# RWKV-7 chunk step of a hybrid decoder: chunk matrices as 64-wide blocks on 64x64 array tiles, and the rotation behind the state update

## The reference

```python
p = p + (shifted - p) * mu                  # shifted: the token before, or the stored state
r, k, v, wl, al, gl = jnp.split(p, B_SPLITS, axis=-1)
w = -jax.nn.softplus(-(w0 + jnp.tanh(wl) @ w2)) - 0.5
decay = jnp.exp(-jnp.exp(w))
a = jax.nn.sigmoid(a0 + al @ a2)
g = jax.nn.sigmoid(gl) @ g2
kk = heads(k * k_k); kk = kk / norm(kk)
k = k * (1.0 + (a - 1.0) * k_a)
b_h = kk * a_h

def step(S, inp):
    r_t, d_t, k_t, v_t, kk_t, b_t = inp
    sa = jnp.einsum('bhij,bhj->bhi', S, -kk_t)
    S = S * d_t[:, :, None, :] + sa[..., None] * b_t[:, :, None, :] + v_t[..., None] * k_t[:, :, None, :]
    return S, jnp.einsum('bhij,bhj->bhi', S, r_t)
```

## Time and profile before

| | |
|---|---|
| median of 3 runs | 3579.61 us |
| the profiled execution's own time | 3578.4 us |
| its span | 3576.6 us |
| granted TensorE clock over the span | 0.969 of full |
| PE busy / DVE / ACT / POOL | 94% / 50% / 33% / 5% |
| HBM traffic | 137 GB/s over the span |

### The profile page before, as it was taken

One profiled execution on the slowest core, in us unless ns is written; L12 is line 12 of the kernel. 1 busy time (PEld: TensorE's weight loads), 2 busy tenths in 40 slices (PEclk: granted clock), 3 DMA queues, 4 the chain that ended last, 5 costly groups with the idle time before them and its releaser, 6 DMA issues.

```text
span 3576.6 us, 57327 instructions
## 1 busy us (share of the span) xinstructions
PE 3367.3 (94%) x23190; PEld 3156.5 (88%) x23190; DVE 1802.5 (50%) x2295; ACT 1192.8 (33%) x1553; POOL 162.1 (5%) x253
## 2 busy tenths in 40 slices
PE   8997888889999999999999978788999999999998
PEld 7996865579999999999999967555999999999998
DVE  5337665145545454454543476742555554545444
ACT  3223117533332232232432231364333233223224
POOL 1002011000000000000000020210000000000000
PEclk9998979999999999999999988799999999999999
DMA  6660005676555555554565500167655555555554
GB/s 190 161 149 5 1 2 197 256 173 146 152 153 143 151 153 139 157 152 137 147 174 151 113 1 1 40 224 263 141 152 152 149 139 159 146 139 161 145 144 128
DMA packets 846373, 490.57 MB, mean 137 GB/s; under 512 B 96352, under 2 KB 822896, under 8 KB 845808
## 3 DMA queue, kind: packets, MB, share of 16 engines
q1 hardware_dynamic: 845804, 488.85, 49.0%
q10 hardware_dynamic: 452, 0.11, 0.0%
HBM read 480.79 MB, written 8.12 MB: 137 GB/s over the span
## 4 chain that ended last, share of the span: by engine, by line
PE 86%; DVE 7%; ACT 3%; issue 1%; DMA 1%; SPq 0%; ACTq 0%; DVEq 0%
PE PS L1317 83%; PE PS L1318 3%; ACT ktr L823 1%; DMA cV<-in_cache_a_v 1%; DVE xm L1022 0%; ACT psm L794 0%; DVE psm L1192 0%; DVE WT L1084 0%; DVE hl L1257 0%; DVE WT L1085 0%; ACT ppt L805 0%; DVE S0T L1171 0%; DVE S0P L1145 0%; DVE nm L1194 0%; DVE xm L1027 0%
## 5 line engine op out<-in xcount | busy, mean ns | idle before, releaser
L625 ACT ACTIVATE wh<-raw 128x2048 fp32r<-128x2048 f32 (+1 forms) x408 | 711.7, 1744 | 1286.0 <-PE PS L1317 1249.9
L900 DVE TENSOR_TENSOR wl<-raw,wh 128x2048 fp32r<-128x2048 f32 (+1 forms) x408 | 848.9, 2081 | 383.8 <-ACT wh L625 383.4
L1317 PE MATMUL PS<-fh,wh 128*128 128x320 f32 x2816 | 870.6, 309 | 0.0
L1317 PE MATMUL PS<-fh,wl 128*128 128x320 f32 x2816 | 870.1, 309 | 0.0
L1317 PE MATMUL PS<-fl,wh 128*128 128x320 f32 x2816 | 870.1, 309 | 0.0
L1317 PE MATMUL PS<-hh,wh 128*128 128x320 f32 x1664 | 517.6, 311 | 22.6 <-DVE hl L1262 17.6
L1317 PEld LDWEIGHTS PS<-fl,wh 128*128 128x128 f32 x2816 | 528.6, 188 | 0.2
L1317 PEld LDWEIGHTS PS<-fh,wh 128*128 128x128 f32 x2816 | 528.6, 188 | 0.2
L1317 PEld LDWEIGHTS PS<-fh,wl 128*128 128x128 f32 x2816 | 528.6, 188 | 0.0
L1317 PE MATMUL PS<-hl,wh 128*128 128x320 f32 x1664 | 516.3, 310 | 0.0
L1317 PE MATMUL PS<-hh,wl 128*128 128x320 f32 x1664 | 516.2, 310 | 0.0
(11 more groups left out here) (328 smaller groups left out, 3044.6 us busy)
## 6 DMA issues: line engine op xcount, KB each, us to landing
raw<-in_w_gate SPq DMA_DIRECT2D x88, 1024.0 KB, 5.6
raw<-in_w_up SPq DMA_DIRECT2D x88, 1024.0 KB, 5.6
raw<-in_w_down SPq DMA_DIRECT2D x128, 704.0 KB, 4.7
raw<-in_w_in SPq DMA_DIRECT2D x56, 1024.0 KB, 5.6
cK<-in_cache_a_k SPq DMA_DIRECT2D x80, 512.0 KB, 6.5
cV<-in_cache_a_v SPq DMA_DIRECT2D x80, 512.0 KB, 8.2
raw<-in_w_in SPq DMA_DIRECT2D x32, 512.0 KB, 5.7
raw<-in_w_out SPq DMA_DIRECT2D x32, 512.0 KB, 4.8
```

The source lines that it names most:

```text
L625: act.activation(wh[j][:, 0:kts], raw[j][:, 0:kts], ACT.Copy).then_inc(sem["wh"], 1)
L900: tt(wl[j][:, 0:kts], raw[j][:, 0:kts], wh[j][:, 0:kts].bitcast(F32), ALU.subtract).then_inc(sem["wl"], 1)
L1317: mm = lambda out, lhsT, rhs, start=True, stop=True: pe.matmul(out, lhsT, rhs, start=start, stop=stop, skip_group_check=True)
```

## The change

Each head's chunk matrix is stored as 64-wide blocks: chunk 0 in partitions 0 to 63, chunk 1 in partitions 64 to 127. So `MT`, `WT`, `TT`, `ET`, `ZZ`, `NTm`, `RBm`, `RKm` have 512 columns in place of 1024, the masks are 64 wide, and a matmul that used the whole array becomes two of 64x64, one for each chunk. In `gram`, TA and Y the four pairs (head half, chunk) fall on four different 64x64 tiles of the array, and the two row halves write to different banks. In the levels (`per_head`), NV and TNV chunk c reads partitions 64c and writes partitions 64c, so the two matmuls fall on the two tiles of the array's diagonal and write to the same bank. The padded copies (`eA`, `eB`, `eR`, `bts`, `kts_`) and their clearing go away; the state update reads 64 rows. The round's first `rotate` stands ahead of U and its second behind the first chunk's state update. On VectorE the last operation of `rotated` comes behind the new state. The token mix `p + (shifted - p) * mu` becomes `p * (1 - mu)` on ScalarE (`mixed`) and one operation per tile on VectorE; GpSimd has no part in it any more.

```diff
+    def both(a):
+        return np.concatenate([a[:HD, :HD]] * 2, 0)
+    put("negE1T", both(-pair(1)))
...
-                pool.tensor_tensor(xv, xv, mu, ALU.mult).then_inc(sem["pool"], 1)
-                pool.tensor_tensor(xv, xv, pT[:, BR + 8:BR + 12], ALU.add).then_inc(sem["xs"], 1)
...
-                pool.memset(eA[:], 0.0)
-                pool.memset(eB[:], 0.0)
-                pool.memset(eR[:], 0.0).then_inc(sem["zero"], 1)
...
+                def mixed(k0, k1):
+                    for k in range(k0, k1):
+                        a = act.activation(xm[:, k], pT[:, BR + k], ACT.Copy, scale=keepmu[:, k:k + 1])
+                    a.then_inc(sem["mixq"], 1)
+                act.wait_ge(sem["ev"], start_of(l, "out"))
+                mixed(12, 14)
+                mixed(4, 8)
...
                 a.then_inc(sem["ksq"], 1)
+                mixed(0, 4)
+                mixed(8, 12)
                 take("z")
...
-                def difference(k0, k1):
-                    done(tt(x[:, :, 1:TOK], p[:, :, 0:TOK - 1], p[:, :, 1:TOK], ALU.subtract))
...
+                def shifted(k0, k1, name):
+                    x, p = xm[:, k0:k1], pB[:, k0:k1]
+                    take("mixq")
+                    ends = sam(x)[:, :, :, 0]
+                    done(tt(edge[:, k0:k1], ends, shmu[:, :, k0:k1].rearrange("p b k -> p k b"), ALU.add))
+                    for k in range(k0, k1):
+                        a = stt(xm[:, k, 1:TOK], pB[:, k, 0:TOK - 1], par[:, MU + k:MU + k + 1], xm[:, k, 1:TOK], ALU.mult, ALU.add)
+                    done(a)
+                    done(dve.tensor_copy(ends, edge[:, k0:k1]), name)
...
-                    for x, y in ((dA, eA), (dB, eB), (dR, eR)):
-                        for h2, rows in enumerate(halves()):
-                            a = dve.tensor_copy(y[rows, :, h2, 0:nt], x[rows, :, c0:c0 + nt])
-                    done(a, "exd")
-                    take("G")
+                    dve.wait_ge(sem["G"], 15 * l + 5 * tau + 2)
+                    done(tt(heads(TT, nt), banks(6, nt), mask("negE1", nt), ALU.mult))
+                    done(tt(heads(TT, nt), heads(TT, nt), mask("eye", nt), ALU.add), "E1")
                     take("Gc")
...
-                            rotated(2 * tau + c)
+                            rotated(2 * tau + c, 0)
                             take("Sm")
                             ps = PS[:, 1, :].rearrange("p (f i) -> p f i", f=4)
                             done(tt(S0P[:], S0P[:], ps, ALU.add))
...
                             done(a, "SP")
+                            rotated(2 * tau + c, 1)
...
                     def gram(b, x, y):
                         for f in range(4):
-                            a = mm(PS[0:nt, b + f // 2, (f % 2) * 2 * nt:(f % 2 + 1) * 2 * nt], x[:, f, cols],
-                                   y[:, f, :, 0:nt])
+                            for h2 in range(2):
+                                r = slice(h2 * HD, h2 * HD + HD)
+                                for c in chunks:
+                                    t = slice(c0 + c * HD, c0 + c * HD + HD)
+                                    a = mm(square(b + h2, f, c), x[r, f, t], y[r, f, t])
                         a.then_inc(sem["G"], 1)
+
+                    def per_head(b, x, y, hs):
+                        for h in hs:
+                            for c in chunks:
+                                a = mm(PS[c * HD:(c + 1) * HD, b, (h - hs[0]) * HD:(h - hs[0] + 1) * HD], head(x, h, c), head(y, h, c))
+                        return a
...
                     take("TAc")
+                    if tau < 2:
+                        rotate(2 * tau)
                     take("tnv")
...
-                            rotate(2 * tau + c)
                             take("Uc")
                             for f in range(4):
                                 fc = slice(f * P, (f + 1) * P)
-                                mm(PS[:, 1, fc], bts[c][:, fc], uu[:, fc], True, False)
-                                a = mm(PS[:, 1, fc], kts_[c][:, fc], vt[:, fc], False, True)
+                                mm(PS[:, 1, fc], bt[r, fc], uu[r, fc], True, False)
+                                a = mm(PS[:, 1, fc], kt_[r, fc], vt[r, fc], False, True)
                             a.then_inc(sem["Sm"], 1)
+                            if c == 0:
+                                rotate(2 * tau + 1)
```

More of the change, by code:

```diff
@@ L242, in build @@
         pc = place("pc", [P, 4, 12], RP + 20480 + 12288)
[L243 removed]
+        MT, WT, TT, ET, ZZ, NTm, RBm = (place(n, [P, 512], RS + 2048 * i) for i, n in enumerate(
             ("MT", "WT", "TT", "ET", "ZZ", "NTm", "RBm")))
@@ L1009, in rotated @@
                 wide = lambda name: C(name).unsqueeze(1).broadcast_to([P, n, TOK])
-                take("rot")
-                tt(y, PS[:, 2:2 + n, 0:TOK] if u % 2 == 0 else PS[:, 5:5 + n, 0:TOK], wide("sin"), ALU.mult).then_inc(sem["rotc"], 1)
-                done(tt(x, x, wide("cos"), ALU.mult))
-                take("rotc")
-                done(tt(x, x, y, ALU.add), "rope")
+                if part != 1:
+                    take("rot")
+                    tt(y, PS[:, turn_bank(u):turn_bank(u) + n, 0:TOK], wide("sin"), ALU.mult).then_inc(sem["rotc"], 1)
+                    done(tt(x, x, wide("cos"), ALU.mult))
+                if part != 0:
+                    take("rotc")
+                    done(tt(x, x, y, ALU.add), "rope")
             def rwkv(l):
@@ L1037, in rwkv @@
                 done(ts(sg13[:], sg13[:], 0.5, 0.5, ALU.mult, ALU.add), "sg")
-                done(difference(0, 4))
-                for k in range(4):
-                    a = shifted(k)
-                done(a, "xrs")
+                shifted(0, 4, "xrs")
+                shifted(8, 12, "xs")
                 xr, xk, xv = xm[:, 0:4], xm[:, 4:8], xm[:, 8:12]
@@ L1083, in rwkv @@
                     take("Gc")
                     done(tt(heads(WT, nt), heads(MT, nt), mask("negE1T", nt), ALU.mult))
-                    done(tt(heads(WT, nt), heads(WT, nt), mask("ident", nt), ALU.add))
-                    take("G")
-                    done(tt(heads(TT, nt), banks(6, nt), mask("negE1", nt), ALU.mult))
-                    done(tt(heads(TT, nt), heads(TT, nt), mask("ident", nt), ALU.add), "E1")
-                    take("G")
+                    done(tt(heads(WT, nt), heads(WT, nt), mask("eye", nt), ALU.add))
@@ L1090, in rwkv @@
+                    dve.wait_ge(sem["G"], 15 * l + 5 * tau + 4)
                     tt(heads(NTm, nt), banks(0, nt), mask("strict" + kind, nt), ALU.mult).then_inc(sem["NT"], 1)
-                    take("G")
                     tt(heads(RBm, nt), banks(2, nt), mask("incl" + kind, nt), ALU.mult).then_inc(sem["RB"], 1)
-                    take("G")
-                    done(tt(heads(RKm, nt), banks(4, nt), mask("incl" + kind, nt), ALU.mult))
+                    dve.wait_ge(sem["G"], 15 * l + 5 * tau + 5)
@@ L1149, in rwkv @@
                     take("Y")
-                    done(dve.tensor_copy(yy[:, :, c0:c0 + nt], PS[:, 0, 0:4 * nt].rearrange("p (f t) -> p f t", f=4)), "Yc")
+                    for c in range(nt // HD):
+                        a = dve.tensor_copy(yy[:, :, c0 + c * HD:c0 + c * HD + HD], PS[:, YB[c], 0:256].rearrange("p (f t) -> p f t", f=4))
+                    done(a, "Yc")
                 own = C("own", NS).unsqueeze(2).broadcast_to([NS, NB, HD])
@@ L1481, in rwkv @@
                                 take("TW")
-                            if not i and not hf:
+                            elif not hf:
                                 take("NT")
```

177 lines of the change are left out of this document (84 added, 93 removed).

## The result

The change makes the kernel 3.0% faster: 3472.32 us (3470.39 to 3477.72, 4 runs) against 3581.9 us for the kernel before (3578.24 to 3585.14, 4 runs), ratio 0.9698, 95% interval 0.9683 to 0.9713. The profiled execution of the change is the slowest of its four (3477.7 us, span 3475.9), that of the kernel before one of the fastest of its own (3578.4 us), so the two traces differ by only 100.7 us.

The account below looks back on a forecast made before the run. TensorE was taken to bound the rounds, VectorE the front part. Rounds 0 and 1 at 8.7 + 23.7 + 22.8 + 1.2 = 56.4 us saved, with round 2, 25.2 and 23.7; front parts 7.4; together 56.3, giving 3523 us, range 3481 to 3552.

Parts of the forecast that it names:

- (a, d): Rounds 0 and 1: start to first TZ, 8.7 us, plus 1.2 for low clock at the next round's transposes.
- (b): Levels of rounds 0 and 1: 26 groups at half clock, 23.7 us against 23.9 before, gain 0.
- (c): Tail of rounds 0 and 1, last subtraction to next round: 22.8 us, with U to U 6.6.
- the clock holds in the levels: Rival: levels stay at full clock, 0.47 us a group, 3481 us for all four rounds; chance 0.20 for some or all.
- The price of four tiles: Gram, TA and Y products: 29 ns a record at either clock, upper bound 57 ns.
- (a): Rounds 0 and 1, start to first TZ: 8.7 us against 16.6, gain 7.9, TensorE idle 1.4.
- (e): Round 2, one chunk and no diagonal pairs: 1.5 us off 40.0, bounds 0 and about 3.
- the slower rival: Diagonal pairs in levels, NV and TNV do not overlap, 107 ns a record: about 3625 us; chance 0.12.
- front part: Token mix ahead of the rounds: 3.7 us less in each layer, bounds 0 and 6.2.

Follow-up runs that it names:

- column pair run: Changed kernel, but in the levels chunk 1's matmul reads chunk 0's 64 rows, so the pair lies on two column halves: 3515.82 us, ratio 0.9826.
- the change's second profile: Profile from running the unaltered changed kernel again beside the variants: 3476.66 us, ratio 0.9703.
- the filler: Changed kernel plus unread 128x128 matmuls in TensorE's two longest waits of a round: 3465.73 us; with the diagonal partner as well: 3457.41 us.
- the reversed edit: Changed kernel with the front part's token mix put back on VectorE and GpSimd: 3480.5 us, ratio 0.972.
- both column runs: Changed kernel with level pairs on two column halves, 3515.82 us; changed kernel with an unread column-half partner in round 2's levels, 3474.48 us.
- the diagonal runs: The changed kernel itself, 3472.32 us and again 3476.66 us; and the changed kernel with the diagonal partner, 3460.12 us.
- the run with two tiles: Changed kernel, but both row halves of a Gram product read partitions 0 to 63, so two tiles are used: 3481.14 us, ratio 0.9715.
- chunk-outer order: Changed kernel, but in the levels all matmuls of chunk 0 of a group are issued before those of chunk 1: 3488.04 us, ratio 0.9742.
- the diagonal partner: Changed kernel, each level matmul of round 2 followed by an unread one on the other diagonal tile: 3460.12 us, ratio 0.9671.

## Why the prediction was wrong in size

The sum was made per round 0 or 1, 56.4 us. Round 0 of layer 0 against it, from the timeline above:

| part | forecast us | measured us |
|---|---|---|
| start to first TZ (a, d) | 8.7 + 1.2 | 9.95 (330.33 to 340.28) |
| first TZ to TA (b, and 0.8 of c) | 24.5 | 15.51 (340.28 to 355.79) |
| TA to first U (c) | 7.8 | 4.83 (355.79 to 360.62) |
| U to U (c) | 6.6 | 6.13 (360.62 to 366.75) |
| second U to next round (c) | 7.6 | 7.77 (366.75 to 374.52) |
| round | 56.4 | 44.19 |

**The clock, step (b), failed.** I wrote "I expect the clock to fall to 1.2 GHz in the first level of each round 0 and 1 ... and to stay there until whole-array work comes". It fell in some of them, after the wait of 2.01 us, and came back among the diagonal pairs. My evidence was one tile, and the earlier trace rows two column halves (the second row holds only some 5 us of levels; NV, TNV, `rotate` and other whole-array work stand behind them); I carried it over to two tiles on the diagonal, for which I had said myself that no row shows them. The column pair run shows that the evidence was right for what it was (17.06 us at 0.50 with TensorE always busy) and the carrying over wrong. Of the 51 us between forecast and result, that run puts 39 on the clock: 24.5 less 15.5 is 9.0 us in the levels of this round, and the low clock reaches into NV, TNV and `rotate` behind them. What happened is the rival to which I gave 0.20, "the clock holds in the levels", with its 0.47 us a group and 3481 us.

The same error is in (c): NV and TNV at 57 ns a record, and `rotate` at 2.2 us for half clock (the terms up to U add up to 8.5 us there, not to 8.6). They took about 1.0 and 1.1 us (at full clock, from 356.30 and 358.27) in place of 1.8 each, and `rotate` 1.27.

**The price of four tiles was mis-sized.** I took 29 ns "at either clock" for Gram, TA and Y, with the argument that four tiles should not be slower at half clock than two at full; that is only an upper bound, and I used it as the price. At half clock it was about right (27 ns: 0.85 us for 32 records from 378.08 of the change, clock 0.50); at full clock it is 15 ns. With 160, 32 and 64 records a round that is up to 256 x 14 = 3.6 us. In (a) VectorE sets the end, so there it only lengthened TensorE's wait (2.01 in place of 1.4 us); in TA and Y it shows. This takes the time below the rival's 3481 us, and so out of the range.

**Round 2, step (e), had the wrong sign.** I took 1.5 us off 40.0 with bounds 0 and 3; it took 41.98 us, and 35 to 36 us once the clock was up. The size of the loss is uncertain. Here are round 2 of layer 1 before and with the change, and of layer 0 in the change's second profile:

```profile
2230.18:2269.29 39.11, 35.11 (x307) 30.48 (x307) 25.16 (x49) 5.12 (x11) 4.40 (x5) 0.83 0.01 1
```
```profile
2129.44:2169.04 39.60, 34.72 (x346) 29.68 (x346) 22.92 (x43) 5.45 (x11) 4.34 (x5) 0.78 0.01 1
```
```profile
417.50:457.95 40.45, 35.58 (x347) 30.75 (x347) 22.92 (x43) 5.44 (x11) 4.35 (x5) 0.75 0.01 1
```

So it was 0.5 to 2 us longer, and with either kernel longer where the granted clock was lower. The saving at its start did not come: the first Z stood 6.2 us behind the round's start in place of 7.6, but then TensorE waited 2.00 us for VectorE, and the first TZ stood at 9.3 us in place of 9.0. The rest of the difference is clock: 20.5 us at 0.50 where before 16.9 were read the earlier trace rows. Why the half clock lasted longer stays open: with the filler in that wait round 2 took 39.6 us, which is also what the change took in layer 1 without it.

**What held.** The diagonal overlaps in one bank: the slower rival (0.12) is refuted by 29 ns a record. The Trainium skill, TensorEngine Tiling (Array Packing), Restrictions and Gotchas, says that different row tiles cannot access the same PSUM bank simultaneously; the trace does not agree for this pair. (a) came out at 9.95 against 9.9. The first two rotation operations fit beside the update as forecast, U to U 6.13 against 6.6. VectorE's operations behind a group stayed hidden: from the first TZ to TA TensorE stood 0.75 us in all (14.76 busy of 15.51), 0.59 of it right ahead of TA. The front part gained 3.7 us in layer 0 as forecast (43.46 to 39.74), but in layer 1 only 2.0 (from the stream's last matmul to round 0, 42.8 to 40.8), where I had put 3.7 again; the reversed edit costs 3.8 us for both layers. Its mechanism is as told: the operations of 3.48 and 2.7 us return with GpSimd's part, and with the change VectorE waits for ScalarE instead:

```profile
299.82 0.21 DVE L1022 TENSOR_TENSOR edge<-xm,shmu 128x32 f32<-128x32 f32 x1 [3.12 <-ACT xm L706]
```

**Busy is not enough.** The rows say that a busy TensorE is not enough for the full clock: 17.06 of 17.06 us busy, at 0.50. The Trainium skill, TensorE: Matmul & The Clock Gate, Part 1, ties the clock to how busy the engine has been; by that rule the change's levels would run at 2.4 GHz, as they did, and so would the column pair's, which did not. Its outcome was the right forecast here and its rule does not cover the two cases beside it.

## What to carry to other kernels

Where small matmuls leave parts of the array idle, look at which tiles they use, not only at how many: 64x64 matmuls in alternating diagonal pairs cost half of a single tile's time and brought the full clock back, while a pair on two column halves overlapped just as well and ran at half clock. If a stretch of one-tile work shows a granted clock of 0.50 and has a free tile on the diagonal, an unread partner cost nothing beside it here (0.49 us for a group at full clock, 0.48 without) and brought the clock back for what followed (12 to 16 us). When pricing a shape that no row shows, do not take the clock from a neighbouring shape without keeping the other clock in the range: the two differ by nearly a factor of two on every record (29 and 57 ns with two tiles, 60 and 107 with one).

## What the hardware showed that I had not expected

- The clock distinguishes layouts at equal count, order and overlap: diagonal pair 1.00 (344.84 to 355.00), column pair 0.50 (341.24 to 358.30, always busy), and a single tile, with half the matmuls, 0.50 (426.80 to 433.31). Whether the diagonal matters because it spans all rows or all rows and all columns was not tried: a pair on two row halves with one column half would tell it. Nor were the operands kept apart from the layout: in both column runs the second tile computes the same product as the first, in the diagonal runs another one.
- A column pair does not lose the clock at once, and work on one column half but all rows (128*64) ran at full clock as well. Here are the Gram products on column pairs in the run with two tiles, and the start of round 2 in the kernel before:

```profile
335.15:338.77 3.62, 3.62 (x131) 3.62 (x128) 2.27 (x4) 0.60 (x1) 1.41 (x2) 1.00 0.02 5
```
```profile
469.16:475.60 6.44, 6.44 (x56) 6.00 (x56) 4.37 (x9) 2.63 (x5) 1.85 (x2) 1.00 0.00 0
```

- Four 64x64 tiles bring the cost of a record to 15 ns, two to 29, where one tile has 60, at full clock.
- Matmuls for a free tile start ahead of earlier ones whose tile is taken, across groups that increment different semaphores: chunk-outer order cost 0.58 in place of 0.46 us a group, not 0.93.
- A wait of 2.5 us ahead of U, in the middle of the tail, was followed by 17.1 us at half clock; with 0.75 us in the same place (the change) none followed in the rest of the round. In the kernel before 2.48 us were followed by none either, so part of what an order of operations saves can be clock, but the wait alone does not decide it.

The best kernel run is the change with the diagonal partner and the filler, 3457.4 us, 3.5% under the kernel before (ratio 0.9649, 0.9636 to 0.9662). Its added matmuls compute nothing that is read; packing round 2's own heads on both tiles of the diagonal would put work in their place. That was not tried.
